# Expert pass of a decoder trunk: 1024-wide chunks, and token rows moved by GpSimd DMA in place of matmuls

## The chip, the cores and the metric

One Trainium2 chip, one of its cores. The metric is the device time in microseconds (us) of one execution of the whole program. Engines: TensorE (PE, matmuls; PEld is its weight load), VectorE (DVE), ScalarE (ACT), GpSimd (POOL), SyncE (SP, which issues the DMAs of the weights).

## The reference

A trunk of two layers over 256 tokens of 1024 features, in float32: a differential attention block with a dense SwiGLU, then a recurrent block with a top-2-of-8 expert SwiGLU, then a norm. The change is in the experts alone:

```python
def moe_swiglu(h, router, wg, wu, wd):
    ...
    top_v, top_i = lax.top_k(logits, TOP_K)
    gates = jax.nn.softmax(top_v, axis=-1)
    comb = jnp.sum(jax.nn.one_hot(top_i, N_EXPERTS, dtype=jnp.float32) * gates[..., None], axis=1)
    out = jnp.zeros_like(t)
    for e in range(N_EXPERTS):
        out = out + comb[:, e:e + 1].astype(t.dtype) * swiglu(t, wg[e], wu[e], wd[e])
```

An expert has gate and up weights of 1024 x 3584 and down weights of 3584 x 1024, 44.04 MB together. Each token goes to two experts of eight. The result is x + out, and the last norm of it.

## The kernel before

**Passes.** The kernel makes one pass per expert over at most 128 of its tokens. An expert with more than 128 tokens gets a further pass; with these inputs there are eight passes in all. Pass 0 is unrolled; passes 1 to 7 are a loop with the same instructions in each engine's stream.

**Precision.** Every float32 operand is split in two parts (`_hi`, `_lo`), and a product is three matmuls, hi x hi, lo x hi and hi x lo (`mm3`, L1152). All matmul operands pass through that.

**Pieces.** Weights come in pieces of 1 MB (128 partitions x 2048 elements). SP loads a piece into one of seven landing slots (L314 to L316, it waits until the piece seven before has been split), ACT copies its hi part into one of four `w_hi` slots (L630, L631, it waits until PE has used the piece that had the slot, `piece_used`), DVE subtracts for `w_lo` (L1071), PE uses it: 12 matmuls of 128 x 512. The table `HALF` (L116) gives the order of the slots: groups of 4 and, twice in a pass of 42 pieces, of 3. In the group behind a group of 3, a piece waits for the one three before it and not four.

**A pass.** Seven chunks of 512 hidden features. Chunk i has two gate pieces into PSUM bank GB, two up pieces into UB, and two down pieces into D0 and D1. Between them ACT applies silu (L640), DVE multiplies (`gated`, L1082), PE transposes four 128 x 128 blocks (`turn_e`, L1474), ACT and DVE split the transposed block (`eT_split_hi` and `eT_split_lo`, L1076). The down pieces of chunk i come one chunk later, before the gate pieces of chunk i + 2. The order is written out by hand on each engine: ACT and DVE take their instructions strictly in order, so that an evacuation stands behind the `hi` or `lo` that is written ahead of it.

**Tokens.** The tokens of the next expert are picked by matmul: `gather` (L1421) multiplies hi and lo parts of all 256 rows by a one-hot matrix, 32 matmuls of 128 x 128, in the last chunk of a pass. The result of a pass (y, 128 tokens x 1024) is split in hi and lo, and `scatter` (L1432) multiplies it by the transposed one-hot matrix, 8 matmuls of 128 x 512, after the gate pieces of the next pass's chunk 0; DVE adds the four products, weighted, to the residual `xres` in SBUF (L1097). GpSimd does nothing in the passes.

## Time and profile before

| | |
|---|---|
| time, median of 3 runs | 1532.12 us (1531.06 to 1533.81) |
| profiled execution | span 1531.7 us, first to last instruction |
| busy | PE 1452.7 us, DVE 1164.9, ACT 938.2, POOL 11.6 |
| expert passes | from 491.8 us to about 1517 us of the span |
| DMA | 427.41 MB, of it 352.3 MB expert weights |

The passes are two thirds of the time. The profiled execution's time is known as its span alone, 0.4 us under the median of the runs; the times below are of that execution. Rows of the timeline begin with the start in us from the span's start and the time taken. Matmuls are pipelined: one of 128 x 512 takes 0.39 us in its row while the next starts 0.227 us later, so a stretch of PE is read from start to start.

### The profile page before, as it was taken

The page shows a single profiled execution, that of the slowest core. Times are in us where ns is not written, and L with a number is a line of the kernel's source. Part 1 is how long each engine was busy: PE and PEld are TensorE (multiplying, and loading weights), DVE is VectorE, ACT ScalarE, POOL GpSimd, SP SyncE. Part 2 cuts the span into 40 slices and gives each one's busy share as a digit, 9 for nine tenths or more (in the row PEclk, how much of TensorE's full clock was granted, in tenths as well). Part 3 has the DMA queues.
Part 4 walks back from the last instruction along what each step waited for, and adds up shares of the span by engine and source line. Part 5 has one row for each costly group of instructions (what it writes and reads, how often), then busy time and mean ns, then how long its engine had stood idle before and what let it go on. Part 6 is the DMA issues. An engine that isn't in the chain of part 4 may idle for free.

```text
span 1531.7 us, 19136 instructions
## 1 busy us (share of the span) xinstructions
PE 1452.7 (95%) x7099; PEld 1215.4 (79%) x7099; DVE 1164.9 (76%) x1047; ACT 938.2 (61%) x778; POOL 11.6 (1%) x30
## 2 busy tenths in 40 slices
PE   5988999999989999999999999999999999999996
PEld 5877788888977778778878877877887887787785
DVE  5667444537675899888879788887888978888786
ACT  4554434434843677667667667766776766776674
POOL 3000000000000000000000000000000000000000
PEclk9998999999998999999999999999999999999999
DMA  9434345662462899899899989989989998998991
GB/s 280 154 110 155 127 172 192 210 222 84 151 242 86 304 335 369 313 352 370 316 333 387 342 329 351 362 313 340 365 311 350 385 344 328 350 363 310 337 370 48
DMA packets 193388, 427.41 MB, mean 279 GB/s; under 512 B 6921, under 2 KB 30049, under 8 KB 193345
## 3 DMA queue, kind: packets, MB, share of 16 engines
q1 hardware_dynamic: 192560, 425.49, 76.6%
q0 software_dynamic: 784, 1.33, 0.5%
q8 instruction: 29, 0.48, 0.1%
q14 instruction: 15, 0.11, 0.0%
HBM read 425.73 MB, written 1.06 MB: 279 GB/s over the span
## 4 chain that ended last, share of the span: by engine, by line
PE 83%; DVE 10%; issue 3%; ACT 3%; DMA 1%; DVEq 0%; SPq 0%; ACTq 0%
PE ps L1157 76%; DVE w_lo L1071 5%; PE ps L1428 2%; PE ps L1474 1%; ACT w_hi L396 1%; DVE w_lo L696 1%; DMA w_ring<-in_attn_w_qkv_dram 1%; PE ps L1211 1%; DVE hn L716 1%; PE ps L1437 1%; PE ps L1438 1%; DVE xres L782 0%; PE ps L1377 0%; DVE work L952 0%; DVE xt_lo L1076 0%
## 5 line engine op out<-in xcount | busy, mean ns | idle before, releaser
L396 ACT ACTIVATE w_hi<-w_ring 128x2048 fp32r<-128x2048 f32 x256 | 486.3, 1915 | 234.4 <-PE ps L1157 224.1
L1157 PE MATMUL ps<-w_hi,xt_hi 128*128 128x512 f32 (+1 forms) x1344 | 535.4, 398 | 28.7 <-DVE xt_lo L1076 18.3
L1157 PE MATMUL ps<-w_lo,xt_hi 128*128 128x512 f32 (+1 forms) x1344 | 525.7, 391 | 0.0
L1157 PE MATMUL ps<-w_hi,xt_lo 128*128 128x512 f32 (+1 forms) x1344 | 525.5, 391 | 0.0
L1071 DVE TENSOR_TENSOR w_lo<-w_ring,w_hi 128x2048 fp32r<-128x2048 f32 x191 | 432.3, 2286 | 65.4 <-ACT w_hi L396 65.0
L1071 DVE TENSOR_TENSOR w_lo<-work,w_hi 128x2048 fp32r<-128x2048 f32 x141 | 320.3, 2287 | 50.1 <-ACT w_hi L396 50.1
L396 ACT ACTIVATE w_hi<-work 128x2048 fp32r<-128x2048 f32 x144 | 275.2, 1917 | 108.8 <-PE ps L1157 108.4
L1157 PEld LDWEIGHTS ps<-w_hi,xt_hi 128*128 128x128 f32 x1344 | 255.7, 190 | 86.1 <-DVE w_lo L1071 25.1
L1157 PEld LDWEIGHTS ps<-w_lo,xt_hi 128*128 128x128 f32 x1344 | 255.9, 190 | 54.2
L1157 PEld LDWEIGHTS ps<-w_hi,xt_lo 128*128 128x128 f32 x1344 | 256.4, 191 | 50.3 <-issue 0.2
L1157 PE MATMUL ps<-w_hi,split 128*128 128x512 f32 x768 | 239.1, 393 | 9.2 <-DVE split L962 4.1
L696 DVE TENSOR_TENSOR w_lo<-w_ring,w_hi 128x2048 fp32r<-128x2048 f32 x65 | 148.1, 2287 | 65.2 <-ACT w_hi L396 65.1
L1157 PEld LDWEIGHTS ps<-w_hi,split 128*128 128x128 f32 x768 | 143.8, 189 | 43.1 <-DVE w_lo L1071 5.2
L1157 PE MATMUL ps<-w_lo,split 128*128 128x512 f32 x384 | 150.0, 390 | 0.0
L396 ACT ACTIVATE split<-ps 128x512 fp32r<-128x512 f32 (+2 forms) x53 | 34.1, 653 | 113.4 <-PE ps L1327 50.0
L1157 PE MATMUL ps<-xt_hi,w_hi 128*128 128x256 f32 x288 | 84.4, 293 | 7.7 <-DVE xt_lo L722 4.9
L1157 PEld LDWEIGHTS ps<-w_lo,split 128*128 128x128 f32 x384 | 72.4, 189 | 15.4
L1157 PE MATMUL ps<-xt_lo,w_hi 128*128 128x256 f32 x288 | 82.6, 287 | 0.0
L1157 PE MATMUL ps<-xt_hi,w_lo 128*128 128x256 f32 x288 | 82.5, 287 | 0.0
L1157 PEld LDWEIGHTS ps<-xt_hi,w_hi 128*128 128x128 f32 x288 | 56.4, 196 | 8.8 <-DVE xt_lo L722 4.2
L1157 PEld LDWEIGHTS ps<-xt_lo,w_hi 128*128 128x128 f32 x288 | 56.5, 196 | 0.1
L1157 PEld LDWEIGHTS ps<-xt_hi,w_lo 128*128 128x128 f32 x288 | 56.4, 196 | 0.0
(226 smaller groups left out, 808.7 us busy)
## 6 DMA issues: line engine op xcount, KB each, us to landing
w_ring<-in_moe_w_up_dram SPq DMA_DIRECT2D x72, 1024.0 KB, 7.0
w_ring<-in_moe_w_down_dram SPq DMA_DIRECT2D x72, 1024.0 KB, 7.1
work<-in_moe_w_gate_dram SPq DMA_DIRECT2D x64, 1024.0 KB, 6.5
w_ring<-in_moe_w_gate_dram SPq DMA_DIRECT2D x48, 1024.0 KB, 7.2
work<-in_moe_w_up_dram SPq DMA_DIRECT2D x40, 1024.0 KB, 7.0
work<-in_moe_w_down_dram SPq DMA_DIRECT2D x40, 1024.0 KB, 6.6
w_ring<-in_attn_w_qkv_dram SPq DMA_DIRECT2D x12, 1024.0 KB, 6.5
w_ring<-in_ffn_w_gate_dram SPq DMA_DIRECT2D x11, 1024.0 KB, 5.1
```

The lines of the kernel that those rows point to most:

```text
L396: return nc.scalar.activation(out, in_, ACT.Copy)
L696: V.tensor_tensor(w_lo[:, half_slot(k), :], land(k), w_hi[:, half_slot(k), :].bitcast(F32), ALU.subtract).then_inc(lo_ready, 1)
L716: V.scalar_tensor_tensor(hn[:, b, :], xres[:, b, :], rstd[:, b:b + 1], gain[:, :], ALU.mult, ALU.mult).then_inc(hn_ready, 1)
L1071: V.tensor_tensor(w_lo[:, half_slot(n), :], land(n), w_hi[:, half_slot(n), :].bitcast(F32), ALU.subtract).then_inc(lo_ready, 1)
L1157: ins = T.matmul(acc, stationary, moving, start=start and k == 0, stop=stop and k == 2)
L1211: T.matmul(ps[:, bank, :], xt_hi[:, 0, 0:P], xt_hi[:, 0:2, :], start=True, stop=True)
L1428: ins = T.matmul(ps[:, bank, P * m:P * m + P], h[:, b, P * c:P * c + P], onehot[:, b, :], start=b == 0, stop=b == NB - 1)
L1437: T.matmul(ps[:, bank, :], onehotT[:, P * b:P * b + P], y_hi[:, o], start=True, stop=False)
L1438: T.matmul(ps[:, bank, :], onehotT[:, P * b:P * b + P], y_lo[:, o], start=False, stop=True).then_inc(sc_ps, 1)
L1474: ins = T.transpose(ps[:, TB, P * s:P * s + P], act_e[:, P * s:P * s + P], ident[:, :])
```

## The change

An expert pass now has four chunks, of 512, 1024, 1024 and 1024 features. A chunk of 1024 has four gate, four up and four down pieces; a gate or up piece of it holds 2 x 128 rows of 1024 columns (4 KB in a row of DRAM, where it was 2 KB), and the products use two PSUM banks each. Its silu, its product, its transpositions and its split are each over 1024 columns. There are 42 pieces in a pass as before, the slots of `w_hi` and the landing slots are the same, and `HALF` is the same table.

The tokens and the results go another way. GpSimd writes the residual and the normed rows to two tensors in DRAM (`x_rows`, `h_rows`) once, before the passes. In each pass PE multiplies the one-hot matrix by a column of token numbers (`slot_tokens`: two matmuls with 2 columns), DVE turns that into row numbers (`slots_in`), and GpSimd fetches 128 rows of `h_rows` (512 KB) by an indirect DMA into `fetched`. PE transposes them (8 blocks), ACT and DVE split them. The result of a pass is evacuated by ACT with its weight (`y_rows`), and GpSimd adds it to `x_rows` by an indirect, accumulating DMA. DVE waits for that DMA (`rows_in_x`) before it overwrites the row numbers, behind the `lo` of piece 9 of the next pass. Only the last pass's result is still scattered by matmul, after SP has loaded `x_rows` back into `xres`. Pass 0's tokens are still gathered by matmul.

Of the removed lines few are shown here; the listing above has them.

```diff
-    EC = FE // CW
+    WIDE = 1024
+    WIDTHS = (CW,) + (WIDE,) * (FE // WIDE)
+    EC = len(WIDTHS)
...
+    COUNT = [w // 256 for w in WIDTHS]
+    FIRST = [sum(WIDTHS[:i]) for i in range(EC)]
+    PASS = 3 * sum(COUNT)
+
+    PLACE, filled = {}, 0
+    for i in range(EC):
+        for stage, k in (("gate", i), ("up", i), ("down", i - 1)):
+            if k >= 0:
+                PLACE[stage, k] = filled
+                filled += COUNT[k]
+    PLACE["down", EC - 1] = filled
...
+
+        def columns(w, i):
+            o, n = FIRST[i], COUNT[i]
+            k = KC // n
+            return [w[e, :, k * q:k * q + k, o:o + WIDTHS[i]] for q in range(n)]
+
+        def rows(i):
+            r = FIRST[i] // P
+            return [md[e, :, r + 2 * q:r + 2 * q + 2, :] for q in range(COUNT[i])]
+
...
+        eT_hi = [split[:, 2048 * k:2048 * k + 1024].rearrange("p (s t) -> p s t", s=8) for k in range(2)]
+        eT_lo = [split[:, 2048 * k + 1024:2048 * k + 2048].rearrange("p (s t) -> p s t", s=8) for k in range(2)]
+        fetched = work[:, 8704:9728]
+        y_rows = work[:, 9728:10752]
...
+        GB, UB, TB, D0 = 0, 2, 4, 6
+        M0, M1 = 4, 5
...
+            sp.wait_ge(rows_in_x, total * 16 + (INIT - 16))
+            sp.dma_start(xres[:, :, :], x_rows[0:S, :].rearrange("(b p) n -> p b n", p=P)).then_inc(x_back, 16)
...
+            pool.wait_ge(x_ready, 6)
+            pool.dma_start(x_rows[0:S, :].rearrange("(b p) n -> p b n", p=P), xres[:, :, :]).then_inc(rows_in_x, 16)
+            pool.dma_start(x_rows[S:S + P, :], xres[:, 0, :]).then_inc(rows_in_x, 16)
+            pool.wait_ge(hn_ready, 8)
+            pool.dma_start(h_rows[0:S, :].rearrange("(b p) n -> p b n", p=P), hn[:, :, :]).then_inc(rows_in_h, 16)
+            pool.dma_start(h_rows[S:S + P, :], hn[:, 0, :]).then_inc(rows_in_h, 16)
+
+            def fetch(p):
+                pool.wait_ge(slot_ok, p + 2)
+                nc.gpsimd.sem_inc(pool_go, 1)
+                nc.gpsimd.indirect_dma_start(out=fetched, out_offset=None, in_=h_rows[:, :],
+                                             in_offset=bass.IndirectOffsetOnAxis(ap=fetch_rows, axis=0),
+                                             ).then_inc(rows_in_h, 16)
+
+            def add_back(p):
+                pool.wait_ge(ys_ok, p)
+                pool.wait_ge(cur_ok, p)
+                pool.wait_ge(rows_in_x, p * 16 + (INIT - 16))
+                nc.gpsimd.sem_inc(pool_go, 1)
+                nc.gpsimd.indirect_dma_start(out=x_rows[:, :],
+                                             out_offset=bass.IndirectOffsetOnAxis(ap=add_rows, axis=0),
+                                             in_=y_rows, in_offset=None, compute_op=ALU.add).then_inc(rows_in_x, 16)
+
+            pool.wait_ge(rows_in_h, INIT)
+            fetch(0)
+            pool.wait_ge(route_ok, 1)
+            total = nc.gpsimd.value_load(passes.bitcast(I32), min_val=E, max_val=E + XP)
+            with nc.gpsimd.Fori(1, total) as p:
+                add_back(p)
+                fetch(p)
...
                 def eT_split_hi(i):
+                    act.wait_ge(et_ps, p * EC + (i + 1))
+                    n = WIDTHS[i] // P
+                    copy(eT_hi[i % 2][:, 0:n, :].rearrange("p s t -> p (s t)"),
+                         ps[:, TB:TB + n // 4, :].rearrange("p a n -> p (a n)")).then_inc(eh_ok, 1)
...
+                    act.wait_ge(piece_used, p * PASS + (P_MOE + PLACE["gate", i] + COUNT[i]))
+                    if not (isinstance(p, int) and i == 0):
+                        act.wait_ge(et_ps, p * EC + i)
+                    n = WIDTHS[i]
+                    nc.scalar.activation(act_e[:, 0:n], ps[:, GB:GB + n // 512, :].rearrange("p a n -> p (a n)"),
+                                         ACT.Silu).then_inc(es_ok, 1)
+
+                hi_run(0, 3)
+                if not isinstance(p, int):
+                    act.wait_ge(piece_used, p * PASS + P_MOE)
+                    act.wait_ge(cur_ok, p)
+                    act.wait_ge(rows_in_x, p * 16 + (INIT - 16))
+                    nc.scalar.activation(y_rows, ps[:, D0:D0 + 2, :].rearrange("p a n -> p (a n)"), ACT.Copy,
+                                         scale=slot_cur[:, 1:2]).then_inc(ys_ok, 1)
+                hi_run(4, 5)
                 silu(0)
+                hi_run(6, 11)
+                silu(1)
+                hi_run(12, 12)
+                eT_split_hi(0)
+                hi_run(13, 21)
+                silu(2)
+                hi_run(22, 22)
+                eT_split_hi(1)
+                hi_run(23, 33)
+                silu(3)
+                hi_run(34, 34)
+                eT_split_hi(2)
+                hi_run(35, 38)
+                eT_split_hi(3)
+                hi_run(39, 40)
+                for j, b in enumerate((GB + 1, UB + 1)):
+                    act.wait_ge(gat_ps, p * 2 + (4 + j + 1))
                     copy(xt_hi[:, 4 * j:4 * j + 4, 0:P],
                          ps[:, b, :].rearrange("p (c t) -> p c t", c=4)).then_inc(gat_hi, 1)
+                hi_run(41, 41)
...
+                def slots_in(bank, count):
+
+                    dve.wait_ge(slot_ps, count)
+                    V.tensor_scalar(spare, ps[:, bank, 0:1], 0.0, spare_row, ALU.is_equal, ALU.mult).then_inc(slot_link, 1)
+                    dve.wait_ge(slot_link, 3 * count - 2)
+                    V.scalar_tensor_tensor(slot_next[:, 0:1], ps[:, bank, 0:1], -1.0, spare, ALU.add,
+                                           ALU.add).then_inc(slot_link, 1)
+                    V.tensor_copy(slot_next[:, 1:2], ps[:, bank, 1:2]).then_inc(slot_link, 1)
+                    dve.wait_ge(slot_link, 3 * count)
+                    V.tensor_copy(fetch_rows, slot_next[:, 0:1]).then_inc(slot_ok, 1)
+
+                lo_run(0, 3)
+                if first:
+                    gate_weights()
+                    V.tensor_copy(member[:, :, 1:2], combs[:, :, 0:1]).then_inc(member_ok, 1)
+                lo_run(4, 6)
                 gated(0)
+                lo_run(7, 8)
+                if first:
+                    slots_in(D0, p + 1)
+                lo_run(9, 9)
+
+                if not first:
+                    dve.wait_ge(ys_ok, p)
+                    dve.wait_ge(rows_in_x, p * 16 + INIT)
+                V.tensor_copy(slot_cur, slot_next)
+                V.tensor_copy(add_rows, slot_next[:, 0:1]).then_inc(cur_ok, 1)
+                V.tensor_copy(member[:, :, 1:2], combs[:, :, bass.ds(p + 1, 1)]).then_inc(member_ok, 1)
+                V.tensor_copy(g_cur.unsqueeze(2), slots[:, :, bass.ds(p + 1, 1)]).then_inc(col_ok, 1)
+                dve.wait_ge(col_ok, p + 1)
+                for b in range(NB):
+                    V.tensor_scalar(onehot[:, b, :], iota_s[:, :], g_cur[:, b:b + 1], None,
+                                    ALU.is_equal).then_inc(oh_ok, 1)
+                lo_run(10, 12)
+                eT_split_lo(0)
+                lo_run(13, 14)
+                gated(1)
+                lo_run(15, 17)
+                slots_in(TB, p + 2)
+                lo_run(18, 22)
+                eT_split_lo(1)
+                lo_run(23, 24)
+                gated(2)
+                for j in range(25, 28):
+                    lo(j)
+                    if first and j - 25 < XP:
+                        further_pass(j - 25)
+                lo_run(28, 34)
+                eT_split_lo(2)
+                lo_run(35, 36)
+                gated(3)
+                lo_run(37, 38)
+                eT_split_lo(3)
+                lo_run(39, 40)
+                for j, b in enumerate((GB + 1, UB + 1)):
+                    dve.wait_ge(gat_hi, p * 2 + (2 + j + 1))
+                    V.tensor_tensor(xt_lo[:, 4 * j:4 * j + 4, 0:P], ps[:, b, :].rearrange("p (c t) -> p c t", c=4),
+                                    xt_hi[:, 4 * j:4 * j + 4, 0:P].bitcast(F32), ALU.subtract).then_inc(gat_lo, 1)
+                lo_run(41, 41)
...
+            def slot_tokens(bank):
+
+                for b in range(NB):
+                    ins = T.matmul(ps[:, bank, 0:2], onehot[:, b, :].bitcast(F32), member[:, b, :],
+                                   start=b == 0, stop=b == NB - 1)
+                ins.then_inc(slot_ps, 1)
...
+                def columns(stage, i, bank):
+                    n, m = COUNT[i], WIDTHS[i] // 512
+                    k = KC // n
+                    for q in range(n):
+                        wh, wl = (w.rearrange("p (c n) -> p c n", c=k) for w in slot(PLACE[stage, i] + q))
+                        for c in range(k):
+                            for half in range(m):
+                                o = slice(512 * half, 512 * half + 512)
+                                ins = mm3(ps[:, bank + half, :], xt_hi[:, k * q + c, 0:P], xt_lo[:, k * q + c, 0:P],
+                                          wh[:, c, o], wl[:, c, o], (q, c) == (0, 0), (q, c) == (n - 1, k - 1))
+                        ins.then_inc(piece_used, 1)
...
+                pe.wait_ge(gat_hi, p * 2 + 2)
+                pe.wait_ge(gat_lo, p * 2 + 2)
+                if not first:
+                    pe.wait_ge(es_ok, p * EC)
+                columns("gate", 0, GB)
+                columns("up", 0, UB)
+
+                pe.wait_ge(es_ok, p * EC + 1)
+                columns("gate", 1, GB)
+                if first:
+                    pe.wait_ge(member_ok, 1)
+                    slot_tokens(D0)
+                turn_e(0)
+                columns("up", 1, UB)
+                pe.wait_ge(el_ok, p * EC + 1)
+                if first:
+                    pe.wait_ge(slot_link, 3)
+                else:
+                    pe.wait_ge(ys_ok, p)
+                down_e(0, 0, COUNT[0])
+                pe.wait_ge(member_ok, p + 2)
+                pe.wait_ge(oh_ok, p * 2 + 4)
+                slot_tokens(TB)
+
+                pe.wait_ge(es_ok, p * EC + 2)
+                columns("gate", 2, GB)
+                pe.wait_ge(slot_ok, p + 2)
+                turn_e(1)
+                columns("up", 2, UB)
+                pe.wait_ge(el_ok, p * EC + 2)
+                down_e(1, 0, COUNT[1])
+
+                pe.wait_ge(es_ok, p * EC + 3)
+                columns("gate", 3, GB)
+                turn_e(2)
+                columns("up", 3, UB)
+                pe.wait_ge(el_ok, p * EC + 3)
+                down_e(2, 0, 2)
+                turn_e(3)
+                pe.wait_ge(rows_in_h, p * 16 + (INIT + 16))
+                for j, bank in enumerate((GB + 1, UB + 1)):
+                    for m in range(4):
+                        c = 4 * j + m
+                        ins = T.transpose(ps[:, bank, P * m:P * m + P], fetched[:, P * c:P * c + P], ident[:, :])
+                    ins.then_inc(gat_ps, 1)
+                down_e(2, 2, COUNT[2])
+                pe.wait_ge(el_ok, p * EC + 4)
+                down_e(3, 0, COUNT[3])
...
+            pe.wait_ge(tail_oh, 2)
+            for b in range(NB):
+                ins = T.transpose(ps[:, TB, P * b:P * b + P], onehot[:, b, :].bitcast(F32), ident[:, :])
+            ins.then_inc(oht_ps, 1)
+            pe.wait_ge(oht_ok, 1)
+            pe.wait_ge(ys_lo, 1)
             scatter()
```

Three places in the instruction streams, as they stand before and after. First ACT, in pass 0, which has the order of every pass. Before, around silu of chunk 1 and of chunk 2; `w_hi` rows are the splits of pieces, `split<-ps` and `xt_hi<-ps` the split of a transposed block, `work<-ps` silu:

```order
L396 ACTIVATE split<-ps 128x512
L640 ACTIVATE work<-ps 128x512
L396 ACTIVATE w_hi<-w_ring 128x2048 x4
L396 ACTIVATE w_hi<-work 128x2048 x2
L396 ACTIVATE xt_hi<-ps 128x4x128
L640 ACTIVATE work<-ps 128x512
```

ACT in the changed kernel, from the splits of pieces 28 to 33 to the end of the last split block:

```order
L456 ACTIVATE w_hi<-w_ring 128x2048 x3
L707 ACTIVATE work<-ps 128x1024
L456 ACTIVATE w_hi<-w_ring 128x2048
L456 ACTIVATE split<-ps 128x1024
L456 ACTIVATE w_hi<-work 128x2048 x3
L456 ACTIVATE w_hi<-w_ring 128x2048
L456 ACTIVATE split<-ps 128x1024
L456 ACTIVATE w_hi<-w_ring 128x2048 x2
L456 ACTIVATE xt_hi<-ps 128x4x128 x2
```

Before, six splits of pieces stand ahead of each split of a block (pieces 10 to 15 here). Now silu comes first, and one piece's split (34) stands between it and the split of the block.

Second PE, before, where the gather stands in the last chunk:

```order
L1157 MATMUL ps<-w_lo,xt_hi 128x512
L1428 MATMUL ps<-split 128x128 [waits es_ok,oht_ok,oh_ok]
L1428 MATMUL ps<-split 128x128 x31
L1157 MATMUL ps<-w_hi,xt_hi 128x512 [waits lo_ready,el_ok]
...
L1157 MATMUL ps<-w_lo,xt_hi 128x512
L1474 MATMUL ps<-ident,work 128x128 [waits el_ok,ea_ok]
L1474 MATMUL ps<-ident,work 128x128 x3
L1157 MATMUL ps<-w_hi,xt_hi 128x512 [waits lo_ready]
```

PE at the same place in the changed kernel, behind the second down piece (35) of chunk 2:

```order
L1261 MATMUL ps<-w_lo,split 128x512
L1589 REGISTER_ALU
L1591 MATMUL ps<-ident,work 128x128 [waits ea_ok]
L1591 MATMUL ps<-ident,work 128x128 x7
L1634 ISA
L1638 MATMUL ps<-ident,work 128x128 [waits rows_in_h]
L1638 MATMUL ps<-ident,work 128x128 x7
L1562 REGISTER_ALU
L1261 MATMUL ps<-w_hi,split 128x512 [waits lo_ready]
```

The 32 matmuls of the gather and the 4 transpositions have become two runs of 8 transpositions, the second of them of the rows that the DMA fetched.

Third DVE in the changed kernel, from piece 7 to piece 12 of pass 0:

```order
L1146 TENSOR_TENSOR w_lo<-work,w_hi 128x2048 x2
L1171 TENSOR_SCALAR small<-ps,small 128x1
L1173 SCALAR_TENSOR_TENSOR small<-ps,small 128x1
L1175 COPY small<-ps 128x1
L1177 CAST small<-small 128x1
L1146 TENSOR_TENSOR w_lo<-work,w_hi 128x2048
L1193 COPY small<-small 128x2
L1194 CAST small<-small 128x1
L1195 COPY small<-small 128x2
L1196 COPY small<-small 128x2
L1199 TENSOR_SCALAR split<-iota_s,small 128x128 x2
L1146 TENSOR_TENSOR w_lo<-w_ring,w_hi 128x2048 x3
```

New are the rows between the `w_lo` rows. In passes 1 to 7 the first four of them stand behind piece 17 instead, and the wait for the adding DMA stands ahead of L1193.

## Rows read from the trace of the kernel before

**Rows 1.** The page's part 1, the whole execution.

```profile
PE 1452.7 (95%) x7099; PEld 1215.4 (79%) x7099; DVE 1164.9 (76%) x1047; ACT 938.2 (61%) x778; POOL 11.6 (1%) x30
```

**Rows 2.** Stages: length, busy us (count) of each engine, clock, DMA share, GB/s.

```profile
607.00:734.00 127.00, 124.03 (x575) 102.19 (x574) 108.39 (x69) 88.19 (x59) 0.00 (x0) 1.00 0.95 348
686.00:716.00 30.00, 30.00 (x137) 24.83 (x137) 27.14 (x16) 21.14 (x14) 0.00 (x0) 1.00 1.04 390
```

**Rows 3.** Timeline (start, us, engine, line): the gather that each pass has.

```profile
607.01 3.68 PE L1428 MATMUL ps<-split 128*128 128x128 f32 x32
...
734.18 3.69 PE L1428 MATMUL ps<-split 128*128 128x128 f32 x32
...
1501.99 3.69 PE L1428 MATMUL ps<-split 128*128 128x128 f32 x32
```

**Rows 4.** Timeline of PE inside one pass; brackets hold idle time and releaser.

```profile
785.63 0.60 PE L1474 MATMUL ps<-ident,work 128*128 128x128 f32 x4
785.99 0.47 PE L1157 MATMUL ps<-w_hi,xt_hi 128*128 128x512 f32 x1
786.30 0.39 PE L1157 MATMUL ps<-w_hi,xt_lo 128*128 128x512 f32 x1
...
791.31 0.39 PE L1157 MATMUL ps<-w_lo,xt_hi 128*128 128x512 f32 x1
793.99 0.49 PE L1157 MATMUL ps<-w_hi,xt_hi 128*128 128x512 f32 x1 [2.29 <-DVE xt_lo L1076]
...
795.95 0.63 PE L1157 MATMUL ps<-w_hi,xt_lo 128*128 128x512 f32 x1
796.38 0.63 PE L1157 MATMUL ps<-w_lo,xt_hi 128*128 128x512 f32 x1
```

**Rows 5.** Timeline of ACT, the same pass.

```profile
789.01 1.92 ACT L396 ACTIVATE w_hi<-work 128x2048 fp32r<-128x2048 f32 x1 [3.99 <-PE ps L1157]
790.84 0.57 ACT L396 ACTIVATE xt_hi<-ps 128x512 fp32r<-128x512 f32 x1
```

**Rows 6.** Timeline of DVE, the same pass.

```profile
756.66 2.72 DVE L1097 SCALAR_TENSOR_TENSOR xres<-ps,small,xres 128x512 f32<-128x512 f32 x4
...
790.96 2.29 DVE L1071 TENSOR_TENSOR w_lo<-work,w_hi 128x2048 fp32r<-128x2048 f32 x1 [3.61 <-ACT w_hi L396]
793.17 0.68 DVE L1076 TENSOR_TENSOR xt_lo<-ps,xt_hi 128x512 fp32r<-128x512 f32 x1
```

**Rows 7.** Groups of instructions by line, 607 to 1502 us.

```profile
L396 ACT ACTIVATE w_hi<-w_ring 128x2048 fp32r<-128x2048 f32 x168 | 318.9, 1916 | 129.9 <-PE ps L1157 129.9
...
L1087 DVE TENSOR_TENSOR split<-ps,split 128x1024 fp32r<-128x1024 f32 x7 | 8.6, 1225 | 15.4 <-ACT split L396 15.4
```

**Rows 8.** Groups of instructions by line, the whole execution.

```profile
L1407 PE MATMUL ps<-rw,work 128*128 128x8 f32 x32 | 5.3, 307 | 1.0 <-DVE work L978 1.0
```

**Rows 9.** Who waited for whom, 607 to 734 us: total, times, longest.

```profile
PE ps L1157 <- DVE xt_lo L1076: 2.3, 1, 2.3
...
PE ps L1157 <- DVE w_lo L1071: 0.4, 1, 0.4
PE ps L1157 <- DVE split L1076: 0.3, 1, 0.3
```

**Rows 10.** SyncE's queue, its waits from 607 to 1500 us.

```profile
SPq L316 <- DVE w_lo L1071: 713.0, 289, 6.3
```

**Rows 11.** Timeline of PE after the last pass.

```profile
1519.81 0.49 PE L1437 MATMUL ps<-split 128*128 128x512 f32 x1 [2.65 <-DVE split L1136]
```

**Rows 12.** DMA issues: count, KB each, median us to landing.

```profile
w_ring<-in_moe_w_down_dram SPq DMA_DIRECT2D x72, 1024.0 KB, 7.1
...
work<-rel_scratch POOLq DMA_DIRECT2D x1, 1024.0 KB, 5.7
...
rw<-in_moe_router_dram POOLq DMA_DIRECT2D x1, 32.0 KB, 10.9
...
rel_scratch<-work POOLq DMA_DIRECT2D x1, 12.0 KB, 4.5
```

More of the change, by code:

```diff
@@ L176, in build_trunk @@
         rw = sb("rw", [P, KC, E])
-        small = sb("small", [P, 376])
+        small = sb("small", [P, 392])
         neg_lam = small[:, 0:1]
@@ L208, in build_trunk @@
         pick = small[:, 344:352]
+        member = small[:, 376:376 + 2 * NB].rearrange("p (b n) -> p b n", b=NB)
+        slot_next = small[:, 380:382]
+        slot_cur = small[:, 382:384]
+        spare_row = small[:, 384:385]
+        spare = small[:, 385:386]
+        fetch_rows = small[:, 386:387].bitcast(I32)
+        add_rows = small[:, 387:388].bitcast(I32)
         qT = work[:, 0:2048].rearrange("p (h t) -> p h t", h=HEADS)
@@ L621, in _ @@
             gathered_hi(0)
-            nc.scalar.sem_inc(es_ok, 1)
             def expert(p):
@@ L1060, in further_pass @@
                     link(ins)
-            V.sem_inc(ea_ok, 1)
-            V.sem_inc(el_ok, 1)
+            V.memset(combs[:, :, E + XP:E + XP + 1], 0.0)
             def expert(p):
+                first = isinstance(p, int)
                 def lo(j):
-                    if isinstance(p, int) and j < HR:
+                    if first and j < HR:
                         return
@@ L1443, in _ @@
             gather(range(4))
-            T.sem_inc(et_ps, 1)
             def expert(p):
+                first = isinstance(p, int)
                 def slot(j):
@@ L1452, in slot @@
                     return w_hi[:, half_slot(n), :], w_lo[:, half_slot(n), :]
-                def up_or_gate(j, bank, half):
-                    wh, wl = (w.rearrange("p (c n) -> p c n", c=4) for w in slot(j))
-                    for c in range(4):
-                        ins = mm3(ps[:, bank, :], xt_hi[:, 4 * half + c, 0:P], xt_lo[:, 4 * half + c, 0:P],
-                                  wh[:, c, :], wl[:, c, :], half == 0 and c == 0, half == 1 and c == 3)
-                    ins.then_inc(piece_used, 1)
@@ new lines, in down_e @@
+                def down_e(i, a, b):
+                    for q in range(a, b):
+                        wh, wl = (w.rearrange("p (s n) -> p s n", s=2) for w in slot(PLACE["down", i] + q))
+                        for m in range(2):
+                            for half in range(2):
+                                o = slice(512 * half, 512 * half + 512)
+                                ins = mm3(ps[:, D0 + half, :], eT_hi[i % 2][:, 2 * q + m, :], eT_lo[i % 2][:, 2 * q + m, :],
+                                          wh[:, m, o], wl[:, m, o], (i, q, m) == (0, 0, 0),
+                                          (i, q, m) == (EC - 1, COUNT[i] - 1, 1))
+                        ins.then_inc(piece_used, 1)
```

222 lines of the change are left out of this document (61 added, 161 removed).

## The prediction

> **What bounds the kernel now.** Read the page's engine shares first: PE is busy for 95% of the span, DVE 76%, ACT 61%, POOL 1% [rows 1]. Then the stages: in one pass PE is busy 124 of 127 us, DVE 108, ACT 88, and the DMA engines stand at 0.95 of their time with 348 GB/s [rows 2]. So DVE and the DMAs are near, but the passes run at PE's pace. Two more views confirm it: ACT's splits of pieces wait for PE to free a slot and never for a landing [rows 7], and SP spends 713 us waiting for DVE to free landing slots, which means that the loads have time to spare [rows 10]. The timeline gives the length of a pass, from one gather to the next: 734.18 - 607.01 = 127.17 us; over seven passes 1501.99 - 607.01 = 894.98, on average 127.85 [rows 3]. What makes up a pass is 504 matmuls of 128 x 512 at 0.227 us (786.30 to 791.31 is 22 of them) [rows 4], 114.5 us. That term doesn't change. The change is worth what it does to the other 13.4 us.
>
> **What goes, per pass.**
> (a) The gather: 32 matmuls in 3.69 us, 0.11 each [rows 3]: 3.5 us of PE.
> (b) The scatter: 8 matmuls at 0.227: 1.8. Two transpositions of the one-hot matrix at 0.11: 0.2.
> (c) The wait inside the pass. PE's next start should be at 791.54 and is at 793.99, 2.45 us later [rows 4]. The reason is on ACT: the split of the piece that waits for a slot (group of three in `HALF`) starts at 789.01 after 3.99 us of idleness, and the split of the transposed block stands behind it, at 790.84 [rows 5]; DVE then finishes that piece's `w_lo` and only at 793.17 the block's lo part [rows 6], for which PE waits. Two short waits, 0.4 and 0.3 of idleness [rows 9], cost 0.16 more each by the measure of the long one (2.29 idle, 2.45 lost): 1.0. The first start after a wait or a turn is another 0.1 late (785.99 to 786.30 is 0.31) [rows 4]. Together 3.7.
> (d) The clock. After the long wait matmuls start 0.43 apart (795.95 to 796.38) [rows 4], the lower of the two clock levels, in some of the passes. The average pass is 127.85 - 127.17 = 0.7 longer than one without it.
> (e) Seven turns become four and one that is longer, each with 0.09 of late start: 0.2.
> Sum 3.5 + 1.8 + 0.2 + 3.7 + 0.7 + 0.2 = 10.1 us.
>
> **What comes, per pass.**
> (f) Eight transpositions of the fetched rows at 0.11: 0.9. The 28 blocks of the activations stay 28.
> (g) Two matmuls of 2 columns. The nearest row is the router's, 8 columns and the same kind of operands: 32 in 5.3 us [rows 8], between 0.17 and 0.31 each; I take 0.2, so 0.4 (0.1 to 0.6).
> (h) New waits. All evacuations now have a block of four pieces (10.9 us) as cover. I followed each with the durations of rows 4 to 7: ACT starts 0.2 us after the piece that frees its slot, w_hi takes 1.9, w_lo 2.3, a block of 1024 takes 1.0 on ACT and 1.2 on DVE [rows 7]. One place is tight, the down pieces of chunk 2. Piece 34 is again one that waits for the piece three before it. From the end of piece 31: ACT at 0.2, DVE's w_lo of 34 from 2.15 to 4.35, block lo part until 5.55, PE at 5.7; PE has two pieces to do, 5.45. It loses 0.25. The product of chunk 3 is then ready 0.15 after PE's piece 35. Total 0.4; bounds 0 (all 0.1 faster than read) and 2.5 (one more split in the way, as today).
> Everything else lies beside PE. DVE loses the four additions of 2.72 us [rows 6], the lo part of y (1.2) [rows 7] and the casts, and gains some 1.1 us of small operations, 108 to about 105 us of 119: covered, with 88% of its time used. The tokens' fetch starts at piece 17 and is needed after piece 35, 50 us later.
> (i) The adding DMA. ACT has y ready 3.2 us after the last piece (`hi` of piece 3 waits for it, then 1.9, then 1.0). DVE comes to the wait behind w_lo of piece 9, whose slot piece 5 frees: 16.3 + 0.2 + 1.95 + 2.3 = 20.8 us after the last piece. Queued behind the wait are the new one-hot matrix and every w_lo from piece 10 on, and PE stops for the latter if DVE is held beyond about 24 us. So it costs nothing up to 21 us from issue to landing and one us per us from there. DMAs of GpSimd landed in 4.5, 5.7 (1 MB) and 10.9 us (many short rows) [rows 12]; none accumulated. I take 0. Two of 10.9 one after the other, for the read and the write, would be 22: 1 us. Below nothing it can't be, since no instruction of the old path starts sooner for it.
> Sum 0.9 + 0.4 + 0.4 = 1.7. Net 8.4 us a pass, so 119.4 us; seven passes: 58.8.
>
> **Pass 0.** It loses (a), (b), (c), (e) and 1.5 us of lower clock: 10.9. It gains (f), twice (g), (h), and two waits of its own. DVE stops at `slots_in` until PE is through gate 1, so w_lo of pieces 9 to 11 come late: 1.4. The bookkeeping of further passes, some 27 operations at 0.2, now stands between pieces 25 to 28 in one go: 1.0. Together 4.5, net 6.4.
>
> **Ends.** Before the passes GpSimd writes 3 MB to DRAM while no weights are loading; nobody waits. After them y is split and scattered as before (PE's first scatter matmul follows 2.65 us of idleness [rows 11]), and the one-hot work fits into that wait. The load of `xres` comes long before. Zero.
>
> Sum: 58.8 + 6.4 = 65.2; span 1531.7 - 65.2 = 1466.5, and with the 0.4 us by which the median lies above the span, 1467 us.
>
> **Can the DMAs follow?** A pass moves 44.04 MB of weights, 0.52 for the fetch, and 1.05 to read and write the added rows: 45.6 MB in 119.4 us is 382 GB/s. Over 30 us the trace shows 390 [rows 2]. At 390 the DMAs need 116.9 us, and seven landing slots smooth the rest: it fits, with 2%. Pieces with rows of 4 KB may go faster, no row here shows 1024-wide gate pieces.
> The Trainium skill speaks against this change: "DMA: Bandwidth & Descriptors", section "Where 436 GB/s comes from", says that for transfers between HBM and SBUF a limit of about 358 GB/s per core binds. By that figure, 45.6 MB would take 127.4 us and the passes would stay as they are, about 1530 us in all. The trace disagrees with it: 390 GB/s over 30 us [rows 2].
>
> **Rivals.**
> 1. The DMAs become the bound. For it: 0.95 of their time at 348 GB/s, so at that share 366 would be the most [rows 2]. A pass would take 124.6, 5.2 more than forecast, eight passes 42: 1509 us; half way, 1488. Against it: the 390 in the same row group, and landings that nobody waits for. Chance 0.15.
> 2. On the slower side, the same resource with a lower rate: the added rows break up the stream of loads, and the rate stays at the 348 GB/s of the pass measured. 45.6 MB take 131 us, 3.2 more than now, eight times: 1557 us. It decides from 357 GB/s downward (45.6 MB in 127.85 us). Chance 0.03.
> 3. The adding DMA comes late. A landing of 25 us costs 4 us in seven passes: 1495; from 30 us there is no gain left, beyond it the kernel is slower. For it: an operation the trace doesn't have, beside full queues, where a load takes 7.1 us [rows 12]. Against it: all its rows are below 11. Chance 0.08, and 0.02 for beyond 30.
> 4. A wait comes back. The order is by hand, and in one of the places of (h) an evacuation could be 2.5 us late, with clock loss behind it, as now. Eight times 2.5: 1487. For it: DVE at 88% and two margins of 0.2. Chance 0.12.
> 5. Fewer waits than I counted, and the small matmuls cheaper: 1460. Chance 0.05.
> The forecast has 0.55.
>
> **Range and chances.** The forecast's own spread, by the bounds of (g) and (h) and a misjudged 0.05 us here or there, is some 7 us either way. Eight in ten: 1458 to 1490, which holds rivals 4 and 5 and half of 1, and leaves out 2 and most of 3. A measurement of this kernel tells 0.2%, 3 us, from no change. Faster by more: 0.93; the same 0.02 (rival 3 near 30 us); slower 0.05 (rival 2 and the end of 3).
>
> **What would show it.** In the trace after, from one set of fetched-row transpositions to the next: 119 to 120 us. PE has no idle time over 0.5 us in a pass and no stretch at the lower clock. The DMAs' rate is over 380 GB/s and ACT's splits still wait for PE alone; if they wait for a landing, rival 1 holds. DVE's first small operation behind piece 9 follows without idleness; if it waits for a DMA, rival 3 holds, and the landing of GpSimd's adding DMA says by how much. A pass over 121 us, or PE waiting for a block's lo part by more than 1 us, would make (h) wrong.

## The result and the profile after

The changed kernel takes 1464.4 us (median of 4 runs, 1463.9 to 1464.6), the kernel before 1532.1 in the same measurement (1531.1 to 1533.8): ratio 0.956, 95% interval 0.955 to 0.957. The forecast was 1467, the range 1458 to 1490.

The page's part 1 for the kernel after (engine, busy us, share of the span, instructions) answers to [rows 1]; its span is 1462.2 us.

```profile
PE 1405.8 (96%) x6865; PEld 1180.5 (81%) x6865; DVE 1137.0 (78%) x1007; ACT 935.3 (64%) x729; POOL 46.9 (3%) x52
```

The span shrank by 69.5 us: PE's busy time by 46.9 and its idle time by 22.6 (79.0 to 56.4). One stage, by the same view as [rows 2]:

```profile
611.00:730.00 119.00, 118.90 (x545) 98.52 (x544) 104.72 (x63) 87.85 (x54) 4.17 (x2) 1.00 0.99 379
```

PE is now busy 118.9 of 119 us, DVE 104.7 (108.4 in 127 before, about 105 forecast). The length of a pass is read from the transpositions of the fetched rows, in PE's timeline (start, us, engine, line):

```profile
834.29 1.04 PE L1638 MATMUL ps<-ident,work 128*128 128x128 f32 x8
```

They start at 595.81, 715.02, 834.29, and so on to 1430.40: seven passes in 834.6 us, 119.18 to 119.27 each. The forecast was 119.4, the mean before 127.85 [rows 3]. All passes are alike now: none has a stretch at the lower clock, where before some had one [rows 4].

The only wait of PE in a steady pass is the tight place of step (h):

```profile
827.34 0.39 PE L1261 MATMUL ps<-w_lo,xt_hi 128*128 128x512 f32 x1
827.83 0.72 PE L1261 MATMUL ps<-w_hi,split 128*128 128x512 f32 x2
828.39 0.40 PE L1261 MATMUL ps<-w_lo,split 128*128 128x512 f32 x1
```

From 827.34 to 827.83 are 0.49 us where 0.23 is the normal distance: 0.26 late, forecast 0.25. ACT and DVE show why, in the same order of work as [rows 5, 6]. First ACT, then DVE:

```profile
822.33 1.92 ACT L456 ACTIVATE w_hi<-w_ring 128x2048 fp32r<-128x2048 f32 x1 [3.52 <-PE ps L1261]
824.15 1.00 ACT L456 ACTIVATE split<-ps 128x1024 fp32r<-128x1024 f32 x1
```

```profile
824.27 2.29 DVE L1146 TENSOR_TENSOR w_lo<-w_ring,w_hi 128x2048 fp32r<-128x2048 f32 x1 [4.06 <-ACT w_hi L456]
826.48 1.22 DVE L1156 TENSOR_TENSOR split<-ps,split 128x1024 fp32r<-128x1024 f32 x1
```

Both engines stand idle for 3.5 to 4 us, waiting for the slot of piece 34, with the finished block lying ready behind it. The lo part is done at 827.7, and PE goes on at 827.83.

The adding DMA, in GpSimd's timeline, and the point on DVE where it would be felt:

```profile
736.28 1.88 POOL L437 DMA_INDIRECT x_rows<-work,small  x1 [73.34 <-ACT work L715]
```

```profile
750.73 2.29 DVE L1146 TENSOR_TENSOR w_lo<-work,w_hi 128x2048 fp32r<-128x2048 f32 x1 [0.42 <-ACT w_hi L456]
752.94 0.16 DVE L1193 COPY small<-small 128x2 f32<-128x2 f32 x1
```

DVE's small operation follows w_lo of piece 9 without a bracket, so it waited for nothing. It stands 16.7 us after the issue. The landings, by the view of DMA issues (columns as in [rows 12]; the last number is the median us to landing):

```profile
w_ring<-in_moe_w_down_dram SPq DMA_DIRECT2D x63, 1024.0 KB, 6.4
...
x_rows<-work,small POOLq DMA_INDIRECT x7, 10.2
work<-h_rows,small POOLq DMA_INDIRECT x7, 8.2
```

The added rows land in 10.2 us: 6.5 us before DVE asks. Last, who waited for whom (total, times, longest), 720 to 1430 us:

```profile
ACT w_hi L456 <- PE ps L1261: 180.0, 192, 3.5
DVE w_lo L1146 <- ACT w_hi L456: 84.8, 120, 4.1
```

ACT's splits of pieces still wait for PE alone, never for a landing, as in [rows 7].

### The profile page after: what moved, and what is told of

Same layout as the page of the kernel before. It is cut to its first block, busy times and chain, and to the rows that moved or that the text cites. A ratio compares the mean times of both kernels' runs of the same rounds, so it can differ in the third digit from the quotient of the medians.

```text
span 1462.2 us, 18423 instructions
## 1 busy us (share of the span) xinstructions
PE 1405.8 (96%) x6865; PEld 1180.5 (81%) x6865; DVE 1137.0 (78%) x1007; ACT 935.3 (64%) x729; POOL 46.9 (3%) x52
## 4 chain that ended last, share of the span: by engine, by line
PE 88%; DVE 6%; ACT 2%; DMA 1%; issue 1%; SPq 0%; DVEq 0%; POOL 0%; ACTq 0%; POOLq 0%
PE ps L1261 83%; PE ps L1591 2%; DVE w_lo L1146 1%; DMA w_ring<-in_attn_w_qkv_dram 1%; DVE w_lo L771 1%; PE ps L1315 1%; DVE hn L791 1%; DVE xres L857 1%; DMA work<-rel_scratch 0%; PE ps L1638 0%; PE ps L1481 0%; ACT w_hi L456 0%; DVE work L1027 0%; PE ps L1511 0%; DVE xt_lo L797 0%
## 5 line engine op out<-in xcount | busy, mean ns | idle before, releaser
L1261 PE MATMUL ps<-w_hi,xt_hi 128*128 128x512 f32 (+1 forms) x1152 | 453.1, 393 | 8.2 <-DVE xt_lo L797 5.9
L1261 PE MATMUL ps<-w_hi,xt_lo 128*128 128x512 f32 (+1 forms) x1152 | 448.1, 389 | 0.0
L1261 PE MATMUL ps<-w_lo,xt_hi 128*128 128x512 f32 (+1 forms) x1152 | 448.0, 389 | 0.0
L1261 PE MATMUL ps<-w_hi,split 128*128 128x512 f32 x1152 | 358.0, 392 | 7.4 <-DVE split L1037 4.1
L1261 PEld LDWEIGHTS ps<-w_hi,xt_hi 128*128 128x128 f32 x1152 | 218.4, 190 | 53.2 <-DVE xt_lo L797 6.6
L1261 PEld LDWEIGHTS ps<-w_hi,split 128*128 128x128 f32 x1152 | 215.6, 188 | 55.4 <-issue 7.9
L1261 PEld LDWEIGHTS ps<-w_lo,xt_hi 128*128 128x128 f32 x1152 | 218.3, 189 | 45.1
L1261 PEld LDWEIGHTS ps<-w_hi,xt_lo 128*128 128x128 f32 x1152 | 218.4, 190 | 43.3 <-issue 0.2
L1261 PE MATMUL ps<-w_lo,split 128*128 128x512 f32 x576 | 224.8, 390 | 0.0
L1261 PEld LDWEIGHTS ps<-w_lo,split 128*128 128x128 f32 x576 | 108.5, 188 | 22.9
```

What stands on the lines that cost most here:

```text
L1261: ins = T.matmul(acc, stationary, moving, start=start and k == 0, stop=stop and k == 2)
```

## The experiments

Theory: a pass runs at PE's pace, and the change's gain is PE work taken away plus waits that its new order avoids. Rival: the DMAs, at 0.99 of their time, set the pass already, or the row DMAs cost something.

**1 and 2. The split of chunk 2's block one piece earlier, or one later.** The edit on ACT (DVE has the same one); experiment 2 puts it behind piece 35:

```diff
+                eT_split_hi(2)
                 hi_run(34, 34)
-                eT_split_hi(2)
```

> The lower row is the changed kernel at 1464.4 us; only the split of the third chunk's transposed block (hi on ACT, lo on DVE) now stands one piece earlier, ahead of piece 34 in place of behind it. Theory PE: a pass runs at PE's pace and its only wait is the 0.26 us (0.36 with the late start behind it) ahead of the down pieces of chunk 2. The block is then there in time, the wait goes in all eight passes: 8 x 0.36 = 2.9, so 1461.5 us, 118.9 a pass. Rival DMA: the DMA engines (0.99 of their time) set the pass already and PE's wait is only where the slack of the loads shows: no change, 1464.4, and 119.2 a pass.

Measured: 1463.2 us (5 runs, 1461.4 to 1465.6), ratio to the kernel before 0.955 (0.954 to 0.957), which the time alone can't tell from the changed kernel. The trace can: seven passes are 119.04 to 119.11 each, so 0.13 went and not 0.36 a pass. PE's wait for the block is gone, and behind it stands another:

```profile
831.31 0.39 PE L1261 MATMUL ps<-w_lo,split 128*128 128x512 f32 x1
831.73 1.09 PE L1591 MATMUL ps<-ident,work 128*128 128x128 f32 x8
```

0.42 where 0.23 is normal: the turn of the last chunk waits for DVE's product (L1165, over at 831.67). That is the 0.15 that step (h) named for this place, and which the first wait had covered in the changed kernel. The rival's "no change" is wrong too.

> The changed kernel with the same split one piece later, behind piece 35, which waits for PE's piece 32. Theory PE, steps (c), (d) and (h) of the prediction: ACT starts w_hi of 35 at 2.9 us after the end of piece 31, DVE ends its w_lo at 7.1 and the block's lo part at 8.3, PE starts at 8.45 where it needs it at 5.45: 3.0 us of wait in place of 0.26, 2.7 more in each of eight passes, 22 us, and lower clock behind the wait in some passes (0.7 on average, 6 in all): 1486 to 1492 us. Rival DMA: the loads set the pass, and a wait of PE inside it is caught up because PE then finds more pieces ready: under 1470 us.

Measured: 1498.0 us (4 runs, 1496.9 to 1498.3), ratio 0.978 (0.976 to 0.979). PE in one pass:

```profile
834.05 0.39 PE L1261 MATMUL ps<-w_lo,xt_hi 128*128 128x512 f32 x1
837.27 0.72 PE L1261 MATMUL ps<-w_hi,split 128*128 128x512 f32 x2 [2.83 <-DVE split L1156]
```

The wait is 2.99 us (837.27 less 834.05, less 0.23), forecast 3.0, and the same in all eight passes. The mean pass is 123.66, so of the 4.4 us added 2.7 are the wait; the clock took the other 1.7, not 0.7. Behind the wait at 959.25 matmuls start 0.43 apart:

```profile
960.26 0.63 PE L1261 MATMUL ps<-w_lo,split 128*128 128x512 f32 x1
960.69 1.05 PE L1261 MATMUL ps<-w_hi,split 128*128 128x512 f32 x2
```

That is the lower level (1.2 GHz). Such stretches stood behind six of the eight waits (not behind the first, nor behind the one at 834.05 shown above), 5 to 13 matmuls long, 1.0 to 2.6 us lost in each. So the miss is in the clock's term alone. That a wait of PE isn't caught up speaks against the DMA rival.

**3. No row DMAs from the second pass on.** The adding DMA's edit; the fetch of passes 1 to 7 is replaced in the same way by a transfer of 2 KB (these passes' results are left out):

```diff
-                nc.gpsimd.indirect_dma_start(out=x_rows[:, :],
-                                             out_offset=bass.IndirectOffsetOnAxis(ap=add_rows, axis=0),
-                                             in_=y_rows, in_offset=None, compute_op=ALU.add).then_inc(rows_in_x, 16)
+                pool.dma_start(step_b, iota_s[:, 0:4]).then_inc(rows_in_x, 16)
```

> The changed kernel where, from the second pass on, the fetch and the adding DMA are each replaced by a transfer of 2 KB to a scratch place in DRAM (the output of these passes is left out, the tokens of pass 1 are used again). 1.57 MB of row traffic a pass and the indirect and adding work are gone. Theory PE, step (i): they cost nothing, 1464.4 us within 1. Rival DMA: the DMA engines set the pass, 44.0 MB in place of 45.6 at 380 GB/s are 4.1 us less a pass, seven passes 29 us: 1435 us. Half way, if the two only meet in a few places: 1450.

Measured: 1463.5 us (5 runs, 1462.1 to 1464.2), passes 119.18 to 119.26. One pass in the stages view:

```profile
720.00:839.00 119.00, 118.90 (x545) 98.53 (x543) 104.67 (x63) 87.81 (x54) 1.08 (x2) 1.00 0.97 369
```

The rate fell from 379 to 369 GB/s, and the pass stayed. The row DMAs are free, as step (i) said.

**4 and 8. Better versions.** The fourth has the edit of experiment 1, the bookkeeping of pass 0 spread (`further_pass` behind pieces 19, 26 and 29), and warm matmuls ahead of pass 0:

```diff
             gather(range(4))
+            for _ in range(4):
+                T.matmul(ps[:, GB, :], h_hi[:, 0, 0:P], h_hi[:, 0, 0:512], start=True, stop=True)
```

The eighth adds on DVE:

```diff
-                lo_run(34, 36)
+                lo_run(34, 35)
                 gated(3)
+                lo_run(36, 36)
```

> The changed kernel with three edits: the split of chunk 2's block one piece earlier (as in the first experiment), the bookkeeping of further passes in pass 0 spread over pieces 19, 26 and 29 in place of 25 to 27, and four matmuls of 512 columns into a free bank after the first gather, so that PE has no idle time before pass 0. Theory PE: 2.9 for the waits, 0.85 for the one wait of pass 0, 1.7 for the lower clock at 491 to 494 us: 1459.0 us. Rival: only the first pass gains, the others run at the pace of the loads: 1461.9 us.

> The kernel of the fourth experiment with one more edit: the product of the last chunk (DVE) stands ahead of w_lo of piece 36 in place of behind it. In the first experiment's trace the pass fell from 119.23 to 119.10 only, since PE then waits 0.24 us at the turn of the last chunk, for that product. Theory PE: this goes too, 118.86 a pass, 8 x 0.24 = 1.9 less than the fourth experiment's 1461.2: 1459.3 us. Rival: w_lo of 36 then comes late by the 1.2 us that the product takes: no gain, or 1 us a pass lost, 1461 to 1469.

Measured: 1461.2 us (5 runs), ratio 0.954 (0.953 to 0.955), and 1460.0 us (5 runs), ratio 0.952 (0.951 to 0.954). The interval of the second lies wholly below that of the changed kernel. The fourth missed its 1459.0 by 2.2: the second wait, which experiment 1 had uncovered, was still there (8 x 0.24 = 1.9). In the eighth's trace the passes are 118.78 to 118.85 (forecast 118.86), with no wait of PE left but five late starts of 0.09 to 0.10 in each. The stretch ahead of pass 0 keeps the full clock, 1.00, where the changed kernel had 0.66 (first the eighth experiment, then the changed kernel; how much of the gain this is stays open, since kernels without the warm matmuls, as that of experiment 11, also have executions without lower clock there):

```profile
490.00:495.00 5.00, 5.00 (x29) 4.16 (x28) 4.42 (x4) 0.08 (x1) 0.00 (x0) 1.00 0.00 0
```

```profile
490.00:495.00 5.00, 4.55 (x13) 3.70 (x14) 4.97 (x6) 0.00 (x0) 0.00 (x0) 0.66 0.24 59
```

**5 to 7. The kernel before, with parts of the change.** Order, on ACT (and the same on DVE):

```diff
-                    for j in range(0 if i > 1 else 1, 6):
+                    for j in range(0 if i > 1 else 1, 5):
                         hi(g0 + j)
                     eT_split_hi(i - 1)
+                    hi(g0 + 5)
```

Fewer matmuls, on PE (`scatter_half` has the four of y_hi, `gather_one` one of 128x128 for each bank):

```diff
-                        scatter()
+                        scatter_half()
-                        gather(range(4))
+                        gather_one()
```

> The kernel before, with nothing of the change but an order: in every chunk the split of the transposed block (hi on ACT, lo on DVE) stands one piece earlier, ahead of the second down piece in place of behind it. Theory order (step c of the prediction): the long wait (2.45 us a pass) and the short one in front of chunk 0's down piece (0.5 with its late start) go, and with them the lower clock behind the long wait (four of eight passes, 1.4 to 1.6 us each): 8 x 2.95 + 6 = 30 us, so 1502 us. Rival: the wait is due to the narrow chunks, whose two down pieces are too short a cover, and moves on to the next piece: 1525 us or more.

> The kernel before, where PE leaves out most of the gather and half of the scatter inside the passes (4 matmuls in place of 32, 4 in place of 8; the gathered tokens are then wrong and y's lo part isn't added). All evacuations and DVE's four additions stay. Theory PE (steps a and b): 28 x 0.11 + 4 x 0.227 = 4.0 us a pass, 32 us in eight: 1500 us. Rival: part of this PE time covers evacuations, and a wait for DVE grows in its place: half, 1516 us.

> The kernel before with both edits, the order and the fewer matmuls. If the two terms are separate they add: 30 + 32 = 62 us, 1470 us, within 6 us of the changed kernel, without a single wide chunk or row DMA. If they cover each other, 1480 us or more. If the DMAs are the bound at the 366 GB/s that 0.95 of their time at 348 GB/s would mean, a pass can't be under 120.3 us and the kernel not under 1471.

Measured (5, 4 and 5 runs), with the mean pass of each trace, from gather to gather (127.85 before):

| kernel | us | ratio, 95% | pass |
|---|---|---|---|
| order | 1500.7 | 0.979 (0.978 to 0.981) | 123.91 |
| fewer matmuls | 1511.8 | 0.987 (0.985 to 0.988) | 125.40 |
| both | 1476.7 | 0.964 (0.963 to 0.965) | 121.02 |

Order alone gives 3.9 us a pass, nearly half of the change's 8.6: the long wait, one of the short ones and all lower clock inside passes go, and the other short wait (0.5) stays. The rival that narrow chunks are too short a cover falls. Fewer matmuls give 2.45 us a pass and not 4.0, near its rival's half. The gather had covered an evacuation; without it PE waits here in every pass:

```profile
736.72 0.72 PE L1157 MATMUL ps<-w_hi,split 128*128 128x512 f32 x2 [0.60 <-DVE split L1076]
```

That is 0.76 us with the start. The short wait for w_lo behind DVE's additions grew from 0.5 to 0.66, and between these marks five of the seven long waits had lower clock behind them, where it was three before: some 0.4 of the 1.55 that is missing. With both edits the pass is 6.8 shorter. The two don't hide each other (the second is worth 2.9 once the order is right), but the new wait (0.83 here) and the grown one (0.66) keep it 7 us above the forecast 1470. Its pass of 121.0 lies above the 120.3 of the DMA rival, so this run doesn't rule that out; the twelfth does.

**9 and 10. The adding DMA made late**, by two or four small transfers ahead of it:

```diff
+                for k in range(2):
+                    nc.gpsimd.sem_inc(pool_go, 1)
+                    pool.dma_start(step_a, iota_s[:, 0:4]).then_inc(slow_step, 16)
+                    pool.wait_ge(slow_step, p * 32 + (16 * (k + 1) - 32))
```

> The changed kernel with two small transfers of GpSimd (2 KB to a scratch place in DRAM), one after the other, ahead of every adding DMA; nothing else differs. Each takes some 5 us, so the added rows land some 20 us after the moment at which the adding DMA is issued now. Step (i) of the prediction: free up to 21 us from issue to landing, so 1464.4 us within 2. By the trace after, DVE comes to its first small operation 16.7 us after that moment, so DVE should show some 3 us of idle time there in each pass, and PE none. Rival: DVE has no slack of its own at that place, and each us of its wait costs one: 3 us in seven passes, 1485.

> The same with four small transfers: landing some 30 us after that moment. Step (i): beyond 21 us one us per us, 9 us in seven passes, 63, and 1 to 2 us of lower clock behind each wait: 1530 to 1542 us, all the gain of the change gone. Rival (more slack than the 21 us, through pieces already split): half, 1495 to 1505.

Measured: 1495.3 us (4 runs, 1490.6 to 1496.7), ratio 0.976 (0.974 to 0.979), and 1559.3 (4 runs), ratio 1.017 (1.014 to 1.020): slower than before the change. Both times were missed, because the small transfers took longer than 5 us each. GpSimd, DVE and PE in one pass of the ninth:

```profile
740.01 0.60 POOL L440 DMA_DIRECT2D step_a<-iota_s  x1 [73.09 <-ACT work L721]
746.59 0.56 POOL L440 DMA_DIRECT2D step_a<-iota_s  x1 [5.98 <-DMA step_a<-iota_s]
753.32 2.47 POOL L443 DMA_INDIRECT x_rows<-work,small  x1 [6.18 <-DMA step_a<-iota_s]
```

```profile
763.82 0.17 DVE L1199 COPY small<-small 128x2 f32<-128x2 f32 x1 [6.84 <-DMA x_rows<-work,small]
```

```profile
767.02 0.50 PE L1267 MATMUL ps<-w_hi,xt_hi 128*128 128x512 f32 x1 [2.96 <-DVE w_lo L1152]
```

DVE goes on 23.8 us after the first issue and PE starts 3.1 late; by "free to 21, then one us per us" it should be 2.8. In the tenth DVE goes on after 32.7 us (750.61 to 783.33), which gives 11.7, and PE is 12.0 late:

```profile
783.33 0.17 DVE L1199 COPY small<-small 128x2 f32<-128x2 f32 x1 [15.76 <-DMA x_rows<-work,small]
```

```profile
786.54 0.80 PE L1267 MATMUL ps<-w_hi,xt_hi 128*128 128x512 f32 x1 [11.88 <-DVE w_lo L1152]
```

In all fourteen passes of the two experiments PE is later than the rule says by the same 0.3 us. So the rule of step (i) holds at two points, and it was the landing that my expectations misjudged. The adding DMA itself landed in 9.4 to 11.2 us in the ninth, but in 6.1 to 6.4 in the tenth, where DVE was held and the loads had nearly stopped (83 GB/s from 777.0 to 783.3): its landing isn't a fixed price. The rest of the time is lower clock again, behind every wait of 10 us or more (1.2 to 2.4 us) and three of the seven of 3 us. The ninth's trace is of its fastest run; the other three were 4 to 6 us longer, and their waits weren't seen.

**11 and 12. More DMA traffic**, two or four transfers of 1 MB more in each pass:

```diff
+                    pool.dma_start(hn[:, :, :], h_rows[0:S, :].rearrange("(b p) n -> p b n", p=P)).then_inc(extra_in, 16)
```

> The changed kernel with two more transfers of 1 MB in every pass (GpSimd reads the token rows from DRAM into an SBUF area that is idle there), one behind the adding DMA and one behind the fetch: 47.7 MB a pass, 400 GB/s in 119.2 us. If the DMA engines can hold only the 379 to 390 GB/s that a pass shows, it takes 122.3 to 125.9 us: 1489 to 1518. If they can hold the 410 GB/s that 1 MB per 2.56 us means (the landings of the gate pieces while the queue is full), 116.3 us are enough and PE stays the bound: 1464.4.

> The same with four such transfers a pass: 49.8 MB, 418 GB/s in 119.2 us, above any rate seen. At 410 GB/s a pass takes 121.5 us: 1483. At 390 it takes 127.7: 1532. If the time stays at 1464 to 1470, the DMAs have more to give than any landing here has shown, and their share of 0.99 says nothing of how near the bound is.

Measured: 1465.9 us (4 runs, 1463.0 to 1467.2), ratio 0.956 (0.954 to 0.959), and 1486.0 (4 runs), ratio 0.970 (0.967 to 0.973). Stages of the eleventh and of the twelfth:

```profile
720.00:839.00 119.00, 118.90 (x544) 98.52 (x543) 104.68 (x63) 87.79 (x54) 5.75 (x4) 1.00 1.02 396
```

```profile
720.00:839.00 119.00, 116.90 (x529) 95.91 (x528) 101.93 (x61) 86.01 (x52) 7.20 (x6) 1.00 1.03 404
```

Two more MB cost nothing (passes of 119.18 to 119.26). With four the DMAs are the bound: all but the first of the passes take 122.0, and ACT now waits for landings:

```profile
ACT w_hi L470 <- PE ps L1275: 69.6, 87, 1.3
ACT w_hi L470 <- DMA w_ring<-in_moe_w_down_dram: 31.7, 24, 2.3
```

49.8 MB in 122.0 us are 408 GB/s; the view's 404 leaves out the read that adding needs. This is what rival 1 would have looked like.

## Why the prediction was right

The mechanism was right in each of its large steps, and the errors of the sum are small. By the medians the forecast is 2.6 us too high, by the spans 4.3 (1466.5 for 1462.2). The difference is luck: the sum put a median 0.4 above the span, but in every run on record an execution's time lies 1.8 to 2.3 above its own span, so the execution profiled before was slower than its median, and this hid 1.7 us of the error. The 4.3 are 1.6 in the seven passes, 1.4 in pass 0 and 1.4 ahead of it.

- **The pass.** 8.6 us against 8.4. Order and waits (steps c and d, 2.45, 1.0 and 0.7 and part of the late starts) were checked by the fifth experiment: 3.9 against the 4.4 of (c) and (d), with one short wait still there. Gather and scatter (a, b) are worth their matmuls only if the evacuations beside them stay covered; the sixth experiment shows 1.55 us less than the matmuls' worth, some 1.0 of it the new and the grown wait and 0.4 clock. In the changed kernel both waits are gone; wide chunks and the missing additions on DVE are the likely cover. From "both" (121.0) to the changed kernel (119.2) another 1.8 us go, of which the two waits of 0.83 and 0.66 give up to 1.5. How much of that is due to the chunks' width and how much to the additions wasn't separated, so the width's own share of the gain is not shown.
- **Step (g).** The slot matmuls stand between 770.84 and 771.20, and the next matmul's late start is 0.1: 0.4 to 0.5, forecast 0.4.
- **Step (h).** 0.26 us for the forecast 0.25. The second wait (0.15) doesn't show, as the first one hides it; experiment 1 uncovered it with 0.19.
- **Step (i).** Right. The landing is 10.2 us, the free time 21, and one us per us from there.
- **Clock (d).** Its size was read from waits of 2.45 us, and holds for these in the kernel before (0.7 a pass). It isn't a price by length of wait: waits of 2.99 us in experiment 2 cost 1.7 a pass, waits of 2.8 to 3.3 in experiment 9 about 0.5.
- **Pass 0.** It gained more than the forecast 6.4. From its first matmul to the fetched rows, and from the last of these to the end, the sum of both stretches shrank by 7.8 us (the mark before is the gather, two pieces later in the pass, which cancels in the sum). The wait for `slots_in`, put at 1.4, was hardly there (0.1), the one for the bookkeeping was 0.85 against 1.0; these two terms are nearly the whole difference.
- **Ends.** Pass 0 began 1.4 us earlier (490.45 against 491.83). The front of the kernel hadn't changed there; the fourth and the eighth experiment, whose fronts are alike, differ by 2.3 us at the fetched rows of pass 0. I take it for variation between executions, which isn't shown. With the 60.4 of seven passes, 7.8 and 1.4 make the span's 69.5.
- **Rate.** "Over 380 GB/s" wasn't met: the view shows 379. The DMA view counts 1.05 MB of row traffic a pass (7.34 MB in seven), so fetch and add once each; the prediction had counted the read that adding needs as well. The need was right to 1%.
- **Rival 1** is refuted with a wide margin. The DMAs hold 404 GB/s when asked, and the pass needs 379, both by the view (408 and 382 with the read that adding needs). A share of 0.95 in [rows 2] didn't mean 95% of what they can do: it is 0.97 at 369 GB/s, 0.99 at 379, 1.02 at 396 and 1.03 at 404. The change also made the loads faster, which the prediction had left open ("may go faster"): in the trace before, landings of gate and up pieces (rows of 2 KB) are mostly 2.71 us apart, 387 GB/s, and those of down pieces (rows of 4 KB) 2.56, 410 GB/s; in the changed kernel all three are mostly 2.56 apart. How near the kernel before was to its own bound no run tests.
  The Trainium skill ("DMA: Bandwidth & Descriptors", section "Where 436 GB/s comes from") lets about 358 GB/s bind between HBM and SBUF, a figure that it works out as a stack's 716 GB/s over two cores. The twelfth experiment's 404 to 408 over whole passes disagree, and the measurement decides for one core alone. What a core gets while its neighbour streams too no run shows: the prediction set against a one-core kernel a figure that is a share of two.
- **Rival 3** has the right wait but too low a price, since it left out the clock: it put 1495 at a landing of 25 us, and experiment 9 was there with 23.5 to 24.0 us; with 31 to 33 us (experiment 10) the kernel is some 27 us slower than before. It didn't happen because the landing has 6.5 us to spare on DVE and 10 on PE.

## What to carry to other kernels

Look at what stands directly behind an instruction that waits for a slot: a finished block behind it is late by the whole wait, and moving one split ahead of it, on ACT and on DVE (experiment 5), was worth nearly half of this large change. Before PE work is removed, ask which evacuation it covers, because that comes out as a wait (experiment 6). For a new wait, compute the free time from issue to use and compare it with landings under load. A DMA share near 1 is no bound while the splits wait for PE; whether the DMAs can give more is told by adding traffic.

## What the runs showed of the hardware

- With rows of 4 KB the DMAs held 404 GB/s by the view (408 with the read that adding needs) over passes of 122 us. In the part of the twelfth experiment's DMA view (720 to 842 us) that gives the rate in slices, most read 408 to 412 GB/s:

```profile
GB/s 406 387 387 387 401 410 410 408 371 282 422 418 410 411 410 411 410 408 410 408 410 408 408 411 411 408 412 410 410 410 410 411 408 410 410 410 408 408 411 410
```

- A piece of 1 MB landed 2.71 us behind the one before it with rows of 2 KB, 2.56 with rows of 4 KB (the most frequent distance of two landings, before and after).
- A 2 KB transfer of GpSimd beside the loads took 5.2 to 6.8 us to land in experiment 9, and the next one started 6.6 us after it; one of 12 KB in the kernel before took 4.5 [rows 12]. An accumulating transfer of 128 rows of 4 KB took 9.9 to 10.6 us beside the loads (after), 6.1 to 6.4 with the loads nearly stopped (experiment 10).
- After an idle time of 2.8 us the granted clock fell to 1.2 GHz in six of eight passes for 5 to 13 matmuls (experiment 2), after 2.3 us in four of eight for 7 to 8 (the kernel before), after some 3.0 us in three of seven (experiment 9), after 9.8 us or more in seven of seven (experiment 10). So the length of the wait alone doesn't decide it, and which pass is hit stays open.
